# Moving one channel group of a causal depthwise convolution from VectorE to GpSimd, and one transpose to another PSUM bank

## The chip, the cores and the metric

The kernel runs on one core of a Trainium2 chip. The metric is the device time of one execution in microseconds (us). Before the change it is 969.46 us, the median of three runs (969.19 to 971.21). All arithmetic is float32.

## The reference, cut to what matters

The program is one sequence of 256 tokens with 1024 features through two blocks. The first has two residual layers: an mLSTM mixer, then attention, each followed by a feed-forward part with a short convolution. The change doesn't touch it. The second block has two layers of this form, and the change is in them:

```python
p = h @ w_in[l]
u_val, u_gate, g_conv, c_q, c_kv, k_idx, w_idx, g_attn = split(p)
# convolution branch, 512 channels
a = u_val * sigmoid(u_gate)
y = conv_general_dilated(a, conv_w, causal, CONV_WIDTH=31, depthwise) + conv_b
y = silu(layernorm(y)) @ w_pw2
# attention branch: an indexer scores every key, top 64 keys are kept
cq = rmsnorm(c_q); q = cq @ w_uq; q_idx = cq @ w_qidx
score = einsum("bth,bths->bts", w_b, relu(q_idx @ k_idx))
_, sel = top_k(score, 64)            # then softmax attention over sel
x = x + gate * rmsnorm(concat([y_conv * silu(g_conv), y_attn * silu(g_attn)]) @ w_out)
```

The depthwise convolution is a sum over 31 taps: for each channel, y[t] = bias + sum over j of w[j] * a[t - 30 + j].

## The kernel before, in words

Every engine has a program of its own, written out by hand; they are ordered only by semaphores (`S(name)`). An activation lies in SBUF with the features on 128 partitions and the 256 tokens along the free dimension, so the 512 convolution channels are four groups (CC = 4) of 128x256 numbers, `b_a[:, c, :]` for the gated input (with 30 columns of zeros ahead) and `b_y[:, c, :]` for the sum.

**The convolution.** ScalarE makes tap 0 with the bias (`tap0`, L897, semaphore `conv0_done`). VectorE makes the other 30 taps of each group, one `scalar_tensor_tensor` each, b_y = b_a shifted * weight column + b_y (`taps`, L2509). Each tap of a group waits for the one before of the same group. `taps((0, 1), 7)` runs seven rounds, and each round issues a tap of group 0 and one of group 1, so that two chains alternate. These calls fill the places between the steps of the attention branch in VectorE's program (from L2540 to L2572), and the last taps of groups 2 and 3 stand between the eight heads of attention.

**The attention branch on the way.** In one layer TensorE's order is: the value and gate products of groups 0 and 1 (`glu`, L1598 and L1617), c_q (L1043), c_kv with the index keys by tokens (L1647) with the sum of squares of c_q between (L1061), then the products of groups 2 and 3 (`glu` again). In the middle of those stands `turn_kidx` (L1627), which turns the 64 index-key features from tokens to features, twice, into PSUM bank 6. Bank 6 is also where the sum of squares of c_q is. VectorE reads it to make the normalised c_q (`b_cqn`, L2551, semaphore `cqn_done`), so `turn_kidx` waits for `cqn_done`. Next come `turn_kv` (L1635), the products of `b_cqn` with w_uq (L1043), the value heads (L1670), the index scores (L1681) and the gate products (L1043, L1700).

VectorE then folds the index scores over heads (L2588), finds the 64 largest per query in 8 rounds (L2597, L2601), and adds masks to the scores of each head (L2610, L2636), which ScalarE exponentiates (L861) and scales (L853) and TensorE turns (L1773). After the last tap VectorE adds the four groups of b_y for the mean (L2660).

**GpSimd** runs four memsets at the start and nothing more. They count up the semaphore `preset`.

**Loads** are issued by SyncE (and a few by ScalarE); no DMA is in the diff.

Of the kernel before, what the change touches and what calls it, by code (L numbers as in the profile page):

```python
# [18 lines left out]
ALU = mybir.AluOpType  # L19
ACT = mybir.ActivationFunctionType  # L20
AX = mybir.AxisListType

P = 128
T = 256
# [3 lines left out]
EPS = 1e-6  # L28
# [6 lines left out]
DEPTH = 2  # L35
D_CONV, TAPS = 512, 31
CC = D_CONV // P
# [5 lines left out]
NEG = -1e30  # L43
# [76 lines left out]
def model(nc, I, out):  # L120
    with ExitStack() as ctx:
# [5 lines left out]
        def S(name):  # L127

            if name not in sems:
                sems[name] = ctx.enter_context(nc.semaphore(name))  # L130
            return sems[name]
# [4 lines left out]
        work = sb("work", [P, 6 * 2048])  # L136
# [5 lines left out]
        ones = sb("ones", [P, T])  # L142
# [5 lines left out]
        sml = sb("sml", [P, 192])  # L148
        mod = sb("mod", [P, DEPTH, 24])
        cact = sb("cact", [P, 8])  # L150
        pb = [ctx.enter_context(nc.psum_tensor(f"bank{i}", [P, 512], F32)) for i in range(8)]

        def W(a, b):
            return work[:, a:b]
# [6 lines left out]
        def col(name, i):  # L161

            return cols[:, bass.ds(COLS[name][0] + i, 1)]

        def three(ap, n):
            return ap.rearrange("p (a b) -> p a b", a=n)

        ident = pc("ident", P)
# [9 lines left out]
        m_gw = W(8192, 8704).rearrange("p (k n) -> p k n", k=DC)  # L178
# [81 lines left out]
        b_kvtok = three(fr[:, 11616:12016], TB)  # L260
# [3 lines left out]
        b_kidx = W(768, 1024)  # L264
# [5 lines left out]
        b_a = W(6144, 6144 + CC * (T + TAPS - 1)).rearrange("p (c t) -> p c t", c=CC)  # L270
        b_y = three(W(7300, 8324), CC)
        b_z = three(W(8324, 9348), CC)
        b_sg = three(W(9348, 9860), 2)
        b_vals = three(W(10240, 11264), TB)
        b_ysq = three(W(0, 1024), CC)
# [25 lines left out]
        def slot(n):  # L301
            return ring[:, place(n), :]
# [80 lines left out]
        def logs(l, i):  # L383

            return 4 + 4 * l + (0, 1, 2, None, 3)[i] + 1

        def root_no(l, i):

            return 7 + 6 * l + (0, 1, 2, None, 3, 4)[i]
# [11 lines left out]
        def _(sp):  # L401
# [47 lines left out]
                    sp.dma_start(slot8(n)[:, wide * m:wide * (m + 1), :], w[:, wide * m:wide * (m + 1), :])                        .then_inc(S(sem), 16)  # L449
            for n in (2, 3):  # L450
                load(n)
            sp.wait_ge(S("preset"), 3)
            w = I["a_w_in"][0].rearrange("(k p) n -> p k n", p=P)
            sp.dma_start(m_gw[:, :, 0:4], w[:, :, 3072:3076]).then_inc(S("gw_in"), 16)
            sp.dma_start(m_gw[:, :, 32:36], w[:, :, 3076:3080]).then_inc(S("gw_in"), 16)
# [72 lines left out]

        @block.gpsimd
        def _(pool):  # L530
            nc.gpsimd.memset(ones[:, :], 1.0).then_inc(S("preset"), 1)
            nc.gpsimd.memset(sml[:, 180:181], EPS).then_inc(S("preset"), 1)
            nc.gpsimd.memset(m_gw[:, :, :], 0.0).then_inc(S("preset"), 1)
            nc.gpsimd.memset(work[0:8, 12160:12288], NEG).then_inc(S("preset"), 1)

        @block.scalar
        def _(act):
# [87 lines left out]
                .then_inc(S("rows_done"), 1)  # L625
            root(0, 1, 1, pb[2][:, 0:T], D)
            act.wait_ge(S("rows_done"), 1)
            act.wait_ge(S("preset"), 4)
            act.dma_start(scratch.ap(), work[0:8, 11904:12288]).then_inc(S("rows_out"), 16)

            def v_first_out(p):
# [244 lines left out]
            def layer(l):  # L876
# [63 lines left out]
                act.wait_ge(S("ln_done"), logs(l, KV))  # L940
                guess(root_no(l, KV), kv_log, kv_root)
                act.wait_ge(S("kv_turned"), 2 * l + 1)
                nc.scalar.activation(b_kidx, pb[6][:, 0:T], ACT.Copy).then_inc(S("kidx_out"), 1)

                tables(SIGMOID)
                for c in range(2):
# [85 lines left out]
        def _(pe):  # L1032
            mm = nc.tensor.matmul
# [36 lines left out]
                return lambda k: pe.wait_ge(S("xg_ready"), base + k + 1)  # L1070


            pe.wait_ge(S("preset"), 1)
            def idle(n):

                for _ in range(n):
# [18 lines left out]
            for k in range(DC):  # L1095
# [5 lines left out]
                for c in range(2):  # L1101
                    last = mm(pb[0][:, T * c:T * (c + 1)], slot8(0)[:, k, P * c:P * (c + 1)], xg[:, k, :],  # L1102
                              start=(k == 0 and c == 0), stop=(k == DC - 1), skip_group_check=True)
            last.then_inc(S("product"), 1)
            pe.wait_ge(S("preset"), 2)
            pe.wait_ge(S("h_ready"), 1)
            for k in range(DC):
                if k % 4 == 0:
# [44 lines left out]
            for c in range(2):  # L1153
                by_features(0, c, K_BANK[c], (2,)).then_inc(S("three_done"), 1)
                last = by_features(0, c, K_BANK[c], (3, 4, 5))
# [6 lines left out]
            for k in range(DC):  # L1162
                o = 64 * (k % 2)
# [414 lines left out]
            def layer(l):  # L1578
# [42 lines left out]
                def turn_kidx():  # L1621

                    pe.wait_ge(S("cq_out"), 5 * l + 5)
                    pe.wait_ge(S("cqn_done"), l + 1)
                    for b in range(TB):
                        for o in (0, 64):
                            last = mm(pb[6][o:o + 64, P * b:P * (b + 1)], b_kvtok[:, b, 128:192], ident,  # L1627
                                      start=True, stop=True, skip_group_check=True)
                    last.then_inc(S("kv_turned"), 1)

# [24 lines left out]
                turn_kv()  # L1655
                arrived(pe, n + 6)
                pe.wait_ge(S("small_in"), 32 * (l + 1))
                w_uq = slot(n + 6).rearrange("p (k n) -> p k n", k=2)
                for m, bank in enumerate((7, 0, 1, 2)):
                    if m in (1, 3):  # L1660
# [164 lines left out]
        def _(dve):  # L1825
# [9 lines left out]
            def after(n):  # L1835
                dve.wait_ge(S("dve_step"), n)

            def then(ins):

                after(link(ins))  # L1840
# [642 lines left out]
            def layer(l):  # L2483
# [16 lines left out]
                def taps(channels, rounds):  # L2500

                    for _ in range(rounds):
                        for c in channels:
                            tap = done_taps[c] = done_taps[c] + 1
                            if tap == 1:
                                dve.wait_ge(S("conv0_done"), CC * l + c + 1)
                            else:
                                after(marks[c])
                            marks[c] = link(v.scalar_tensor_tensor(  # L2509
                                b_y[:, c, :], b_a[:, c, tap:tap + T], col("conv_w_2", 124 * l + 4 * tap + c),  # L2510
                                b_y[:, c, :], ALU.mult, ALU.add))
# [25 lines left out]
                if l == 0:  # L2537
                    modulation(1, 4, 6)
                    layer_gains(1)
                taps((0,), 4)  # L2540
                glu_raw(1)
                taps((0, 1), 6)

                dve.wait_ge(S("cq_out"), 5 * l + 1)
                v.tensor_tensor(sq[:, 1, :], sq[:, 1, :], sq[:, 0, :], ALU.add).then_inc(S("sum_done"), 1)
                taps((0, 1), 7)
                mean_square(logs(l, CQ), pb[6][:, 0:T], ms[:, 0:T], 256)
                newton(root_no(l, CQ), ms[:, 0:T], rbc, nwt[:, 0:T])
                dve.wait_ge(S("cq_out"), 5 * l + 2)
# [1 line left out]
                    ins = v.scalar_tensor_tensor(b_cqn[:, c, :], b_cq[:, c, :], col("q_norm_g_2", 2 * l + c), rbc,  # L2551
                                                 ALU.mult, ALU.mult)
                ins.then_inc(S("cqn_done"), 1)
                taps((0, 1), 7)
                dve.wait_ge(S("cq_out"), 5 * l + 5)
                v.tensor_scalar(wcol, b_kvtok[:, :, 192:200], IDX_HEADS ** -0.5 * D_IDX ** -0.5, None, ALU.mult)\
                    .then_inc(S("wcol_done"), 1)
# [3 lines left out]
                    ins = v.tensor_scalar(kv_diag[:, b, :], ident, kv_root[:, b:b + 1], None, ALU.mult)  # L2561
                ins.then_inc(S("kvn_done"), 1)
                glu(2)
                taps((0, 1, 2), 4)
                taps((0, 2), 2)
                taps((1, 2), 2)
                glu(3)
                dve.wait_ge(S("kv_turned"), 2 * l + 2)
                v.tensor_scalar(b_kvn, pb[5][:, 0:T], col("kv_norm_g_2", l), None, ALU.mult).then_inc(S("kvn_done"), 1)
                taps((1, 3), 4)  # L2570
                taps((2, 3), 7)
                taps((3,), 3)  # L2572
                dve.wait_ge(S("wcol_done"), l + 1)
# [53 lines left out]
                for n_head in range(8):  # L2627
                    if n_head < 8:
                        h = 8 * (1 + l) + n_head
                        dve.wait_ge(S("am_done"), 4 * l + n_head // 2 + 1)  # L2630
                        dve.wait_ge(S("scores_done"), h + 1)
                        if n_head >= 2:
                            dve.wait_ge(S("exp_done"), 2 * (h - 1))
                        x, at = sc_sb[n_head % 2], 136 + 2 * (n_head % 2)
                        for b, (lo, hi) in enumerate(((0, P), (P, DIAG))):
                            ins = v.tensor_tensor_reduce(x[:, lo:hi], pb[n_head % 2][:, lo:hi], am[:, n_head, lo:hi],  # L2636
                                                         -KV_LORA ** -0.5, 3.4e38, ALU.add, ALU.min,
                                                         sml[:, at + b:at + b + 1])
                        ins.then_inc(S("max_done"), 1)
                    if n_head < 8 and n_head % 2 == 0 and n_head < 6:  # L2640
                        masked_bias(n_head // 2 + 1)
                    if n_head == 0:
                        reciprocals(0)
                        taps((2, 3), 1)
                    elif n_head < 5:
                        taps((2, 3), 2)
                        if n_head == 4:
                            gate_attention(0)
                        reciprocals(n_head)
                    elif n_head < 7:  # L2650
                        if n_head == 6:
                            gate_attention(1)
                        taps((2, 3), 2)
                        reciprocals(n_head)
                        taps((2, 3), 1)
                    else:
                        taps((3,), 1)
                        reciprocals(7)
                        after(marks[3])
                        then(v.tensor_tensor(b_ysq[:, 0:2, :], b_y[:, 0:2, :], b_y[:, 2:4, :], ALU.add))  # L2660
                v.tensor_tensor(b_ysq[:, 0, :], b_ysq[:, 0, :], b_ysq[:, 1, :], ALU.add)\
                    .then_inc(S("sum_done"), 1)
                gate_attention(2)
                assert done_taps == [TAPS - 1] * CC
                dve.wait_ge(S("ss_done"), sums_on_pe(l, MEAN))
                mean = pb[2][:, 0:T].unsqueeze(1).broadcast_to([P, CC, T])
                v.scalar_tensor_tensor(b_yn, mean, -1.0 / D_CONV, b_y, ALU.mult, ALU.add)\
# [111 lines left out]
```

## Time and profile before

| | |
|---|---|
| median of 3 runs | 969.46 us |
| the profiled execution, its own time | 971.52 us |
| its span, first to last instruction | 969.7 us |
| mean granted TensorE clock | 0.998 |
| first of the two layers | from about 690 us to 829 us |
| second | from about 829 us to the end |

Times in the rows further down are microseconds from the start of the span. PE is TensorE, DVE VectorE, ACT ScalarE, POOL GpSimd. The end of a matmul is modelled, and successive matmuls overlap, so a group's start-to-start distance says more than its end: 16 matmuls of 128x256 take 3.45 us from one group's start to the next, though each group is shown with 3.62. The same holds for VectorE: a tap is shown with some 0.48 us, but 14 taps of two alternating groups take 5.62.

### The profile page before, as it was taken

To read this page: it belongs to the slowest core of one execution; us is meant where nothing else is said; L and a number is where in the kernel's file an instruction comes from. 1 tells how busy PE (TensorE), PEld (TensorE's weight loads), DVE (VectorE), ACT (ScalarE), POOL (GpSimd) and SP (SyncE) were. 2 spreads that over 40 slices of the span, in tenths; PEclk is the share of its full clock that TensorE was granted. 3 is DMA by queue.
4 is the path that set the end of the run, shared out by engine and by line. 5 is a ranking of instruction groups with operands and counts; after the bars stand their busy time and mean duration, and the time that the engine had idled before them with its cause. 6 is when DMAs were issued, how large, how long until landed. Compare 5 with 4: busy or idle time off the path is not lost.

```text
span 969.7 us, 15791 instructions
## 1 busy us (share of the span) xinstructions
PE 960.0 (99%) x6003; PEld 871.1 (90%) x6003; DVE 723.1 (75%) x1551; ACT 276.4 (29%) x603; POOL 1.1 (0%) x8
## 2 busy tenths in 40 slices
PE   9999999999999999999999999999999999999997
PEld 8888999999999988888999999999888878888876
DVE  5578777876887489757678778875799972799963
ACT  2133112112111222253121121112433363634561
POOL 0000000000000000000000000000000000000000
PEclk9999999999999999999999999999999999999999
DMA  9891566766776240685357677762753512543201
GB/s 276 276 290 50 180 209 199 264 235 221 256 260 237 70 148 1 193 262 196 122 192 265 216 244 251 270 209 92 227 170 130 163 44 84 190 136 107 63 1 44
DMA packets 132952, 170.72 MB, mean 176 GB/s; under 512 B 8723, under 2 KB 120483, under 8 KB 132771
## 3 DMA queue, kind: packets, MB, share of 16 engines
q1 hardware_dynamic: 131155, 167.69, 52.7%
q10 hardware_dynamic: 1744, 2.32, 0.7%
q8 instruction: 34, 0.56, 0.2%
q14 instruction: 19, 0.16, 0.0%
HBM read 168.93 MB, written 2.64 MB: 177 GB/s over the span
## 4 chain that ended last, share of the span: by engine, by line
PE 95%; DVE 4%; ACT 1%; issue 0%; DVEq 0%; POOL 0%; POOLq 0%
PE bank L1391 26%; PE bank L1404 16%; PE bank L1043 9%; PE bank L1714 5%; PE bank L1501 5%; PE bank L1130 4%; PE bank L1367 3%; PE bank L1700 3%; PE bank L1137 3%; PE bank L1327 3%; PE bank L1617 2%; PE bank L1598 2%; DVE work L2509 2%; PE bank L1054 1%; PE bank L1541 1%; PE bank L1102 1%
## 5 line engine op out<-in xcount | busy, mean ns | idle before, releaser
L1404 PE MATMUL bank<-work,fring 128*128 128x256 f32 x704 | 155.6, 379 | 0.0
L1404 PEld LDWEIGHTS bank<-work,fring 128*128 128x128 f32 x704 | 132.1, 190 | 17.0
L2280 DVE SCALAR_TENSOR_TENSOR work<-work,cols 128x256 f32<-128x256 f32 x176 | 71.6, 479 | 53.2 <-ACT work L723 53.2
L2509 DVE SCALAR_TENSOR_TENSOR work<-work,cols 128x256 f32<-128x256 f32 x240 | 98.8, 477 | 1.0 <-ACT work L897 0.5
L1391 PE MATMUL bank<-sq,fring 128*128 128x128 f32 x640 | 84.5, 275 | 0.0
L723 ACT ACTIVATE work<-work,cols 128x256 f32<-128x256 f32 x88 | 45.6, 589 | 122.1 <-DVE work L2259 100.7
L1391 PE MATMUL bank<-sq,ring 128*128 128x128 f32 x640 | 78.0, 275 | 0.0
L1391 PE MATMUL bank<-ring,fring 128*128 128x128 f32 x640 | 78.0, 275 | 0.0
L1391 PEld LDWEIGHTS bank<-sq,fring 128*128 128x128 f32 x640 | 77.9, 192 | 0.0
L1391 PEld LDWEIGHTS bank<-ring,fring 128*128 128x128 f32 x640 | 76.2, 192 | 1.0
L1391 PEld LDWEIGHTS bank<-sq,ring 128*128 128x128 f32 x640 | 74.7, 192 | 0.0
L2295 DVE SCALAR_TENSOR_TENSOR work<-work,cact 128x1536 f32<-128x1536 f32 x32 | 58.1, 1815 | 0.6
L1714 PE MATMUL bank<-ring,fring 128*128 128x256 f32 x256 | 57.8, 380 | 0.0
L1714 PEld LDWEIGHTS bank<-ring,fring 128*128 128x128 f32 x256 | 48.3, 190 | 6.7 <-issue 0.3
L717 ACT ACTIVATE work<-bank 128x128 f32<-128x128 f32 x40 | 10.8, 275 | 149.5 <-PE bank L1391 149.5
L2256 DVE TENSOR_TENSOR work<-work,bank 128x256 f32<-128x256 f32 x40 | 16.8, 421 | 35.2 <-PE bank L1391 34.2
L1043 PE MATMUL bank<-work,ring 128*128 128x256 f32 x192 | 42.4, 379 | 0.0
L1043 PE MATMUL bank<-xg,ring 128*128 128x256 f32 x192 | 42.3, 380 | 0.0
L1391 PE MATMUL bank<-ring 128*128 128x128 f32 x320 | 42.3, 275 | 0.0
L1043 PEld LDWEIGHTS bank<-xg,ring 128*128 128x128 f32 x192 | 36.3, 190 | 5.1
L1043 PEld LDWEIGHTS bank<-work,ring 128*128 128x128 f32 x192 | 36.3, 190 | 4.9
L1391 PEld LDWEIGHTS bank<-ring 128*128 128x128 f32 x320 | 38.9, 192 | 0.0
(408 smaller groups left out, 1605.5 us busy)
## 6 DMA issues: line engine op xcount, KB each, us to landing
fring<-in_f_w_up SPq DMA_DIRECT2D x44, 1024.0 KB, 7.5
work<-in_w_ada SPq DMA_DIRECT2D x32, 768.0 KB, 6.1
fring<-in_f_w_down SPq DMA_DIRECT2D x22, 1024.0 KB, 5.0
ring<-in_w_in SPq DMA_DIRECT2D x18, 1024.0 KB, 5.3
ring<-in_a_w_in SPq DMA_DIRECT2D x10, 1024.0 KB, 11.8
ring<-in_w_kv SPq DMA_DIRECT2D x8, 1024.0 KB, 7.2
ring<-in_w_out SPq DMA_DIRECT2D x8, 1024.0 KB, 5.1
ring<-in_a_w_out SPq DMA_DIRECT2D x4, 1024.0 KB, 9.9
```

The lines of the kernel that those rows point to most:

```text
L723: nc.scalar.activation(f_t[v][:, c, :], f_u[:, v, c, 0:T], ACT.Identity, bias=col(f"f_conv_b{f}", n), scale=col(f"f_conv_w{f}", n)).then_i ...
L1043: last = mm(bank[:, T * c:T * (c + 1)], w[:, k, at + P * c:at + P * (c + 1)], x[:, k, :], start=(k == 0), stop=(k == nk - 1))
L1130: last = mm(dst, w[:, k, P * c:P * (c + 1)], x[:, k, :], start=(k == 0), stop=(k == 3))
L1137: last = mm(dst, x[:, k, :], w[:, k, :], start=(k == 0), stop=(k == 3))
L1327: last = mm(bank[:, P * at:P * (at + 1)], w[:, k, P * c:P * (c + 1)], side[:, k, :], start=(k == 0), stop=(k == 3))
L1391: last = mm(bank[:, P * at:P * (at + 1)], w[:, k, P * c:P * (c + 1)], x[:, k, :], start=(k == 0), stop=(k == 3))
L1404: last = mm(pb[m // 2][:, T * (m % 2):T * (m % 2 + 1)], w[:, k, P * m:P * (m + 1)], f_act[:, par, T * k:T * (k + 1)], start=(first and k = ...
L1501: last = mm(places[n], x[:, k, :], w[:, k, :], start=(k == 0), stop=(k == 3))
L1714: last = mm(bank[:, 0:T] if apart else bank[:, T * m:T * (m + 1)], y2[:, k, P * b:P * (b + 1)], slot8(load)[:, k, :], start=(k == 4 and (m ...
L2280: ins = v.scalar_tensor_tensor(f_t[q][:, c, :], f_u[:, q, c, tap:tap + T], col(f"f_conv_w{f}", 44 * tap + n), f_t[q][:, c, :], ALU.mult, A ...
L2295: ins = v.scalar_tensor_tensor(acc, f_ada[:, half, :], k, acc, ALU.mult, ALU.add)
L2509: marks[c] = link(v.scalar_tensor_tensor(b_y[:, c, :], b_a[:, c, tap:tap + T], col("conv_w_2", 124 * l + 4 * tap + c), b_y[:, c, :], ALU.m ...
```

## The change

Four edits.

1. GpSimd takes all 30 taps of group 0 in each of the two layers. It has no one-instruction form of a tap here: it multiplies the shifted input by the weight column, broadcast along the tokens, into a scratch row `b_tap`, and adds that to `b_y[:, 0, :]`. Each of the two waits for the other before it. It starts when ScalarE has made tap 0 of group 0. VectorE waits for the last of them ahead of the sum for the mean.
2. VectorE's calls of `taps` lose group 0. Where it stood alone the call is gone; where it stood beside group 1, group 1 now runs alone; two taps of group 1 move ahead.
3. `turn_kidx` writes to bank 4 instead of 6, ScalarE copies from there, and the wait for `cqn_done` moves from `turn_kidx` to the first product that reads `b_cqn`.
4. The semaphore `preset` is called `pool_done`, and goes on counting.

```diff
+        b_tap = W(11920, 12176)
+        def pool_taps(l, tap):
+            return 4 + 2 * (TAPS - 1) * l + 2 * tap
...
+            for l in range(DEPTH):
+                pool.wait_ge(S("conv0_done"), CC * l + 1)
+                for tap in range(1, TAPS):
+                    if tap > 1:
+                        pool.wait_ge(S("pool_done"), pool_taps(l, tap - 1))
+                    nc.gpsimd.tensor_tensor(b_tap, b_a[:, 0, tap:tap + T],
+                                            col("conv_w_2", 124 * l + 4 * tap).broadcast_to([P, T]),
+                                            ALU.mult).then_inc(S("pool_done"), 1)
+                    pool.wait_ge(S("pool_done"), pool_taps(l, tap) - 1)
+                    nc.gpsimd.tensor_tensor(b_y[:, 0, :], b_y[:, 0, :], b_tap, ALU.add).then_inc(S("pool_done"), 1)
...
                 act.wait_ge(S("kv_turned"), 2 * l + 1)
-                nc.scalar.activation(b_kidx, pb[6][:, 0:T], ACT.Copy).then_inc(S("kidx_out"), 1)
+                nc.scalar.activation(b_kidx, pb[4][:, 0:T], ACT.Copy).then_inc(S("kidx_out"), 1)
...
                     pe.wait_ge(S("cq_out"), 5 * l + 5)
-                    pe.wait_ge(S("cqn_done"), l + 1)
...
-                            last = mm(pb[6][o:o + 64, P * b:P * (b + 1)], b_kvtok[:, b, 128:192], ident,
+                            last = mm(pb[4][o:o + 64, P * b:P * (b + 1)], b_kvtok[:, b, 128:192], ident,
...
                 pe.wait_ge(S("small_in"), 32 * (l + 1))
+                pe.wait_ge(S("cqn_done"), l + 1)
...
-                taps((0,), 4)
                 glu_raw(1)
-                taps((0, 1), 6)
+                taps((1,), 6)
...
-                taps((0, 1), 7)
+                taps((1,), 7)
                 mean_square(logs(l, CQ), pb[6][:, 0:T], ms[:, 0:T], 256)
...
-                taps((0, 1), 7)
+                taps((1,), 7)
                 dve.wait_ge(S("cq_out"), 5 * l + 5)
...
                 glu(2)
-                taps((0, 1, 2), 4)
-                taps((0, 2), 2)
-                taps((1, 2), 2)
+                taps((1, 2), 8)
                 glu(3)
...
-                taps((1, 3), 4)
+                taps((1, 3), 2)
+                taps((3,), 2)
                 taps((2, 3), 7)
                 taps((3,), 3)
...
                         after(marks[3])
+                        dve.wait_ge(S("pool_done"), pool_taps(l, TAPS - 1))
                         then(v.tensor_tensor(b_ysq[:, 0:2, :], b_y[:, 0:2, :], b_y[:, 2:4, :], ALU.add))
```

## Rows read from the trace of the kernel before

**Rows 1.** The page: busy time, share of the span and instructions of each engine.

```profile
PE 960.0 (99%) x6003; PEld 871.1 (90%) x6003; DVE 723.1 (75%) x1551; ACT 276.4 (29%) x603; POOL 1.1 (0%) x8
```

**Rows 2.** TensorE's waits, whole span: who waited for whom, total, times, longest.

```profile
PE bank L1627 <- DVE work L2551: 1.2, 1, 1.2
...
PE bank L1773 <- ACT sq L853: 0.6, 2, 0.3
```

**Rows 3.** TensorE in order of time: start, duration, line, tile, shape, count [idle before].

```profile
714.15 0.59 PE L1061 MATMUL bank<-sq,ones 128*128 128x256 f32 x2
...
717.29 3.62 PE L1598 MATMUL bank<-xg,ring 128*128 128x256 f32 x16
722.08 0.66 PE L1627 MATMUL bank<-consts,fring 128*64 128x128 f32 x8 [1.18 <-DVE work L2551]
...
733.14 0.61 PE L1635 MATMUL bank<-ms,fring 128*128 128x128 f32 x4
733.58 7.07 PE L1043 MATMUL bank<-work,ring 128*128 128x256 f32 x32
...
858.03 3.62 PE L1598 MATMUL bank<-xg,ring 128*128 128x256 f32 x16
861.75 0.66 PE L1627 MATMUL bank<-consts,fring 128*64 128x128 f32 x8
```

**Rows 4.** ScalarE in order of time, first layer.

```profile
700.64 0.58 ACT L897 ACTIVATE work<-work,cols 128x256 f32<-128x256 f32 x1
...
718.01 0.50 ACT L934 ACTIVATE fring<-bank 128x400 f32<-128x400 f32 x1
...
746.92 1.08 ACT L967 ACTIVATE fring<-bank 128x512 f32<-128x512 f32 x2 [0.88 <-PE bank L1681]
```

**Rows 5.** VectorE in order of time, first layer.

```profile
704.81 2.05 DVE L2509 SCALAR_TENSOR_TENSOR work<-work,cols 128x256 f32<-128x256 f32 x4
...
713.35 0.41 DVE L2545 TENSOR_TENSOR sq<-sq 128x256 f32<-128x256 f32 x1
713.69 5.62 DVE L2509 SCALAR_TENSOR_TENSOR work<-work,cols 128x256 f32<-128x256 f32 x14
...
721.06 0.88 DVE L2551 SCALAR_TENSOR_TENSOR work<-work,cols,rstd 128x256 f32<-128x256 f32 x2
721.85 5.62 DVE L2509 SCALAR_TENSOR_TENSOR work<-work,cols 128x256 f32<-128x256 f32 x14
...
728.25 0.48 DVE L2561 TENSOR_SCALAR ms<-consts,sml 128x128 f32<-128x128 f32 x2
...
747.89 0.48 DVE L2588 SCALAR_TENSOR_TENSOR fring<-fring,consts 128x256 f32<-128x256 f32 x1
...
752.14 0.35 DVE L2588 SCALAR_TENSOR_TENSOR fring<-fring,consts 128x128 f32<-128x128 f32 x1
```

**Rows 6.** The taps (L2509) by stretch: length, VectorE busy (count), granted clock, DMA.

```profile
700.00:748.00 48.00, 36.35 (x89) 1.00 0.49 154
839.00:888.00 49.00, 36.33 (x89) 1.00 0.46 151
...
766.00:790.00 24.00, 13.04 (x31) 1.00 0.34 108
```

**Rows 7.** GpSimd's instructions by form: busy, mean ns.

```profile
L533 POOL MEMSET work<- 128x512 f32 x1 | 0.5, 524 | 0.0
L531 POOL MEMSET ones<- 128x256 f32 x1 | 0.3, 312 | 0.3 <-POOLq L2767 0.3
```

**Rows 8.** The first layer's attention in order of time: TensorE, ScalarE, VectorE.

```profile
773.52 0.49 PE L1773 MATMUL bank<-consts,sq 128*128 128x128 f32 x3
...
790.96 0.55 PE L1773 MATMUL bank<-consts,sq 128*128 128x128 f32 x3 [0.31 <-ACT sq L853]
...
771.98 0.80 ACT L853 ACTIVATE sq<-sq,sml 128x128 f32<-128x128 f32 x2 [0.15 <-DVE sml L2625]
...
789.96 0.67 DVE L2660 TENSOR_TENSOR work<-work 128x512 f32<-128x512 f32 x1
```

More of the change, by code:

```diff
@@ L451, in _ @@
                 load(n)
-            sp.wait_ge(S("preset"), 3)
+            sp.wait_ge(S("pool_done"), 3)
             w = I["a_w_in"][0].rearrange("(k p) n -> p k n", p=P)
@@ L530, in _ @@
         def _(pool):
[L531 to L534, printed above, removed]
+            nc.gpsimd.memset(ones[:, :], 1.0).then_inc(S("pool_done"), 1)
+            nc.gpsimd.memset(sml[:, 180:181], EPS).then_inc(S("pool_done"), 1)
+            nc.gpsimd.memset(m_gw[:, :, :], 0.0).then_inc(S("pool_done"), 1)
+            nc.gpsimd.memset(work[0:8, 12160:12288], NEG).then_inc(S("pool_done"), 1)
+            for l in range(DEPTH):
[8 more added lines that the diff above has]
+                    nc.gpsimd.tensor_tensor(b_y[:, 0, :], b_y[:, 0, :], b_tap, ALU.add).then_inc(S("pool_done"), 1)
         @block.scalar
@@ L627, in _ @@
             act.wait_ge(S("rows_done"), 1)
-            act.wait_ge(S("preset"), 4)
+            act.wait_ge(S("pool_done"), 4)
             act.dma_start(scratch.ap(), work[0:8, 11904:12288]).then_inc(S("rows_out"), 16)
@@ L1070, in xg_ready @@
                 return lambda k: pe.wait_ge(S("xg_ready"), base + k + 1)
-            pe.wait_ge(S("preset"), 1)
+            pe.wait_ge(S("pool_done"), 1)
             def idle(n):
@@ L1104, in _ @@
             last.then_inc(S("product"), 1)
-            pe.wait_ge(S("preset"), 2)
+            pe.wait_ge(S("pool_done"), 2)
             pe.wait_ge(S("h_ready"), 1)
@@ L2663, in layer @@
                 gate_attention(2)
-                assert done_taps == [TAPS - 1] * CC
+                assert done_taps == [0] + [TAPS - 1] * 3
                 dve.wait_ge(S("ss_done"), sums_on_pe(l, MEAN))
```

## The prediction, made before the changed kernel ran

> **What bounds the kernel now.** I start at the busy times. TensorE is at 99% and VectorE at 75% [rows 1], and a quarter of free VectorE time might tempt one to look there; but with TensorE full, an edit can give back only TensorE's waits. So the second view is TensorE's waits. In the two layers that the change touches there are three kinds. One is the wait of `turn_kidx` for the normalised c_q, once, 1.2 us. Another is a wait of the head transposes for ScalarE, 0.6 us over two places [rows 2]. The third, between the layers and at the end, waits on the output norm and isn't touched.
>
> The third view is TensorE in order of time, because a wait shown after a modelled end is a little too short. In the first layer L1598 starts at 717.29, and 16 matmuls take 3.45 from start to start, so `turn_kidx` could start at 720.74. It starts at 722.08: 1.34 us are lost. In the second layer it could start at 861.48 and starts at 861.75: 0.27 lost [rows 3]. That is all the time that edit 3 can give: 1.6 us.
>
> VectorE's order of time tells why it can matter though it is not full. Its taps run without a gap to 747.89, where folding the index scores starts [rows 5]; ScalarE's first relu, which that step needs, started at 746.92 and holds two of 0.54 [rows 4]. So VectorE reaches the index about 0.4 us after its input is there. From there the top-64 search and the eight heads follow at once. In the heads TensorE turns a head at 773.52 that ScalarE finished scaling at 772.78 [rows 8]. So VectorE may be late at the index by some 0.7 us, and each further microsecond makes TensorE wait. VectorE is a second bound, hidden under the first.
>
> **The change, part by part.** The rename (edit 4) costs nothing: the same counts at the same instructions.
>
> *Edit 3, the other bank.* Without the wait for `cqn_done`, `turn_kidx` needs only the copy of c_kv, which ends at 718.51 [rows 4], before 720.74. Bank 4 was read before that copy. The moved wait stands ahead of the product at 733.58 (732.24 once the stall is gone) [rows 3]; b_cqn is ready at 721.94 [rows 5], so 10 us cover it. Behind it on TensorE stand all later products, so if the cover went, each microsecond would count in full. Gain: 1.34 + 0.27 = 1.6 us, if all else keeps pace.
>
> *Edit 2, what VectorE saves.* 89 taps stand ahead of the index in each layer [rows 6]; 30 of them go. Two prices are needed. A tap in a single chain costs 0.51 (2.05 for 4), a tap in alternating chains 0.40 (5.62 for 14) [rows 5]. Before: 4 single, and 12, 14, 14, 20 and 25 alternating. After: 0, then 6, 7 and 7 single, 16 alternating, and 23 of which 2 are newly single. Savings: 2.0; 4.8 - 3.1 = 1.7; 5.6 - 3.6 = 2.0 twice; 8.0 - 6.4 = 1.6; 10.0 - 9.4 = 0.6. In sum 9.9 us a layer. Alone they bring almost nothing: VectorE would wait for groups 2 and 3 and then for the relu, whose time TensorE sets. The 31 shown in the attention stretch stay.
>
> *Edit 1, GpSimd's own time.* 60 instructions a layer, each waiting for the one before. The trace has no such instruction; the nearest are memsets, 0.312 us at 256 columns and 0.524 at 512 [rows 7], or 0.10 fixed and 0.21 per 256 columns of one stream. Estimate: at least 0.31 (all streams at once), at most 0.73 (two read and one written in turn); I take 0.52, the two reads in turn, and 0.1 for the semaphore step. The chain starts at about 701.2, when tap 0 is made [rows 4], and is needed at 789.96 [rows 8]: 88.8 us for 60, or 1.48 each. Even 0.73 plus the step stays under it; undisturbed, the chain ends near 701.2 + 60 * 0.62 = 738. The wait added on VectorE (behind it: the mean, the layer norm, the last gates) should cost nothing.
>
> *Edit 1, what it does to VectorE.* This is the disputed term. Every tap on VectorE reads two tensors from SBUF, and so do most other instructions between 701 and 748. Nothing in this trace has both engines busy in SBUF. Bound from below: 0, if they don't disturb each other. Bound from above, 0.73 - 0.13 = 0.60 us for each GpSimd instruction: VectorE stands for all of the slowest one, less what it can hide. The 0.13 comes from VectorE's prices: 0.48 at 256 columns and 0.35 at 128 [rows 5] make 0.27 of streaming in the 0.40 of a tap, so 0.13 of each tap is not streaming. With my 0.52 the price is 0.39.
>
> The trace shows only that GpSimd has been silent beside VectorE [rows 7]. The Trainium skill (SBUF — State Buffer, "Who interferes with whom") says that a VectorE instruction with two SBUF inputs contends with a GpSimd instruction that reads SBUF, and "SBUF: two separate sides" calls it an exclusive lock for the whole instruction. No row here shows it. By that rule the sum is the 0.39 to 0.60 case below; without it the 0 case. The skill's GPSIMD Engine Reference, "Elementwise — side-by-side cycle accounting", has about 2.6 cycles an element for two inputs; 256 of them at 1.2 GHz would be an estimated 0.55 us, beside my 0.52.
>
> At what price does the loss begin? 9.9 us saved, over up to 60 instructions that fall ahead of the index, is 0.165 us each. Any disturbance above a sixth of a microsecond makes VectorE later at the index than now. I think some disturbance likely, since a tap needs two streams at once from a memory whose access the two engines might share, and take turn-taking as likeliest. The sum per layer: some 6 of the 60 fall beside VectorE instructions that read at most one SBUF tensor (reduces, bank reads, some 5.5 us), leaving 54 * 0.39 = 21.1; the 20 single taps already had 0.12 of waiting each that this fills, -2.4; less 9.9 saved; less the 0.7 that the heads lend. That leaves 8.1 us late, and twice that is 16 us. TensorE waits for it ahead of the heads, so the 1.6 us of edit 3 are swallowed there. 971.5 + 16 = 987.5 for the profiled execution; its own time stood 2 us over the median, so I predict 985.5.
>
> **On the way** the same price would show at two places earlier. The sum of squares (L2545) has 17 disturbed instructions ahead: +6.6 - 3.7 saved = 716.2 instead of 713.35, and TensorE needs it at 714.15 [rows 3, 5], a wait of over 2 us. kv_diag (728.25 plus 0.4) would come near 736, needed at 733.14. Both stalls only anticipate the one at the index.
>
> **The rivals.**
>
> *A. No disturbance.* For: nothing in the rows speaks of one. Then VectorE has b_cqn at about 719 and waits for TensorE at groups 2 and 3, edit 3 gives its 1.6 us, and the head stalls (0.47 each: eight matmuls of 0.216 from 788.76 leave TensorE free at 790.49, it starts at 790.96 [rows 8]) stay, as they come from the heads' own chain. 969.5 - 1.6 = 967.9; with both head stalls 967.0.
>
> *B. A mild disturbance, each slowed a bit.* At 0.1 us each VectorE still reaches the index in time, giving 968; at 0.3, 54 * 0.3 - 2.4 - 9.9 - 0.7 = 3.2 us a layer, or 976. I put the case at 968 to 980.
>
> *C. VectorE keeps the path and GpSimd starves.* Back-to-back taps leave it only gaps. It decides from 1.48 us per GpSimd instruction; at 1.8 the chain ends 19 us late, less some 8 us of products that cover it: +11 a layer, 991. Against it: VectorE's dependent single taps leave a gap after every one.
>
> *D. Turn-taking at the upper price, 0.60:* 54 * 0.60 - 2.4 - 9.9 - 0.7 = 19.4 a layer, 1008.
>
> **Chances.** Turn-taking at about 0.39, D with it: 0.45. C: 0.07. B: 0.23 (above the 0.2% bound 0.10, within it 0.10, below 0.03). A: 0.25 (faster by over 0.2%, which is 1.9 us and about what a measurement of this kernel can tell from no change, 0.11; within it 0.14, since 1.6 lies just inside). So faster 0.14, same 0.24, slower 0.62. Most chance lies on one side, but A is a quarter, so the range must reach it: 966.8 to 1008, leaving out half of D. The likeliest case's own range is 976 to 1008.
>
> **What would show it.** Right: L2509's mean between 705 and 760 grows from 0.48 to 0.7 or more while POOL is busy and falls back once POOL is done; the index (L2588) starts some 9 us later relative to L1681; a new wait of TensorE for VectorE of about 8 us ahead of or in the heads. The GpSimd chain ends well before L2660. Edit 3 is right if L1627 has no wait and the wait at the b_cqn product is nil. Wrong: L2509 at 0.48 with POOL busy (then A), or VectorE waiting ahead of L2660 for POOL (then C). A VectorE gap ahead of groups 2 and 3 would also speak for A.

## The result, and the profile after

The changed kernel takes 991.02 us (median of 4, 989.56 to 992.26) beside 970.34 us for the kernel before in the same session (969.19 to 971.33): a ratio of 1.0208 with a 95% interval of 1.0191 to 1.0226, or 20.2 us of 970.34 (the two medians are 20.7 apart). The forecast was 985.5 us, in a range from 966.8 to 1008, and slower. Its profiled execution has a span of 987.8 us, but the layers began 2.4 us earlier in that execution than in the one before (the first product of the layer at 687.76 instead of 690.19), before anything of the change has run. Counted from the start of the layers the difference is 987.8 - 969.7 + 2.4 = 20.5 us.

The page of the changed kernel, part 1, against [rows 1]: TensorE has much the same work, VectorE has 60 instructions less and 18 us **more** busy time.

```profile
PE 963.5 (98%) x6003; PEld 872.1 (88%) x6003; DVE 741.1 (75%) x1491; ACT 276.5 (28%) x603; POOL 88.3 (9%) x128
```

Part 5 of the same page, three of its groups. A tap (L2525, formerly L2509) is now 0.632 us on the mean of the whole kernel instead of 0.48:

```profile
L546 POOL TENSOR_TENSOR work<-work,cols 128x256 f32<-128x256 f32 x60 | 40.3, 672 | 803.5 <-ACT work L913 798.9
...
L2525 DVE SCALAR_TENSOR_TENSOR work<-work,cols 128x256 f32<-128x256 f32 x180 | 105.3, 632 | 3.2 <-ACT work L913 1.3
...
L550 POOL TENSOR_TENSOR work<-work 128x256 f32<-128x256 f32 x60 | 46.8, 781 | 4.7
```

TensorE's waits, against [rows 2]. The wait at `turn_kidx` is gone. A larger one has come, at the c_q products, for VectorE's gating of the fourth group (L2532):

```profile
PE bank L1059 <- DVE work L2532: 14.6, 2, 7.4
...
PE bank L1059 <- DVE mod L2209: 0.7, 1, 0.7
...
PE bank L1059 <- ACT hT L922: 0.5, 1, 0.5
```

TensorE in order of time, first layer and then the same place of the second, against [rows 3]. L1642 is `turn_kidx`; it follows at once. L1059 at 731.02 is the product of c_q with w_uq: 24 matmuls run, then TensorE stands for 7.37 us, and the last 8 take 3.58 from start to start where 8 took 1.73:

```profile
719.37 0.66 PE L1642 MATMUL bank<-consts,fring 128*64 128x128 f32 x8
...
730.48 0.71 PE L1650 MATMUL bank<-ms,fring 128*128 128x128 f32 x4
731.02 5.34 PE L1059 MATMUL bank<-work,ring 128*128 128x256 f32 x24
743.73 3.78 PE L1059 MATMUL bank<-work,ring 128*128 128x256 f32 x8 [7.37 <-DVE work L2532]
747.31 4.12 PE L1059 MATMUL bank<-work,fring 128*128 128x256 f32 x16
751.27 1.88 PE L1686 MATMUL bank<-fring,work 128*128 128x512 f32 x4
...
881.16 5.34 PE L1059 MATMUL bank<-work,ring 128*128 128x256 f32 x24
893.69 3.78 PE L1059 MATMUL bank<-work,ring 128*128 128x256 f32 x8 [7.19 <-DVE work L2532]
897.27 4.24 PE L1059 MATMUL bank<-work,fring 128*128 128x256 f32 x16
901.34 1.88 PE L1686 MATMUL bank<-fring,work 128*128 128x512 f32 x4
```

The reason for those slow 8 is in the windows of the two stretches after the waits (length, busy of PE, PEld, DVE, ACT, POOL, then the granted clock): 0.70 and 0.69 of full speed on the mean, so part of each at the lower level, 1.2 GHz, after TensorE had stood for 7 us. It was 1.00 at the same work before [rows 6].

```profile
743.00:752.00 9.00, 8.27 (x26) 6.66 (x27) 8.93 (x19) 3.79 (x7) 3.71 (x6) 0.70 0.36 116
893.00:902.00 9.00, 8.31 (x26) 6.72 (x27) 8.93 (x19) 3.72 (x7) 3.67 (x6) 0.69 0.35 116
```

VectorE in order of time, first layer, against [rows 5], and then GpSimd beside it:

```profile
706.28 4.88 DVE L2525 SCALAR_TENSOR_TENSOR work<-work,cols 128x256 f32<-128x256 f32 x6 [0.67 <-ACT work L913]
711.08 0.95 DVE L2560 TENSOR_TENSOR sq<-sq 128x256 f32<-128x256 f32 x1
711.96 5.68 DVE L2525 SCALAR_TENSOR_TENSOR work<-work,cols 128x256 f32<-128x256 f32 x7
...
729.50 0.92 DVE L2576 TENSOR_SCALAR ms<-consts,sml 128x128 f32<-128x128 f32 x2
730.34 0.41 DVE L2532 TENSOR_TENSOR work<-bank,work 128x256 f32<-128x256 f32 x1
730.68 12.67 DVE L2525 SCALAR_TENSOR_TENSOR work<-work,cols 128x256 f32<-128x256 f32 x16
743.27 0.41 DVE L2532 TENSOR_TENSOR work<-bank,work 128x256 f32<-128x256 f32 x1
743.60 0.47 DVE L2582 TENSOR_SCALAR work<-bank,cols 128x256 f32<-128x256 f32 x1
743.99 11.53 DVE L2525 SCALAR_TENSOR_TENSOR work<-work,cols 128x256 f32<-128x256 f32 x23
755.44 0.48 DVE L2602 SCALAR_TENSOR_TENSOR fring<-fring,consts 128x256 f32<-128x256 f32 x1
```

```profile
731.09 0.67 POOL L546 TENSOR_TENSOR work<-work,cols 128x256 f32<-128x256 f32 x1
731.84 0.79 POOL L550 TENSOR_TENSOR work<-work 128x256 f32<-128x256 f32 x1
732.70 0.68 POOL L546 TENSOR_TENSOR work<-work,cols 128x256 f32<-128x256 f32 x1
...
746.31 0.79 POOL L550 TENSOR_TENSOR work<-work 128x256 f32<-128x256 f32 x1
```

Seven single-chain taps take 5.68 us, 0.81 each; sixteen in alternating chains take 12.67, 0.79 each; a pair of GpSimd instructions starts every 1.61, 0.81 each. The two engines run in lock step in these stretches, one tap to one GpSimd instruction, whatever the chain. The gating at 730.34, one of whose inputs is in PSUM, keeps its 0.41 in the middle of it. Once GpSimd is through (746.31 + 0.79 = 747.1), the taps are back at 0.40 and the top-64 search and the heads are as before. The index starts 67.7 us after the layer's first product, where it started 57.7 after (747.89 - 690.19): 10.0 us late.

### The profile page after: what moved, and what is told of

Same layout as the page of the kernel before. It is cut to its first block, busy times and chain, and to the rows that moved or that the text cites. A ratio compares the mean times of both kernels' runs of the same rounds, so it can differ in the third digit from the quotient of the medians.

```text
span 987.8 us, 15857 instructions
## 1 busy us (share of the span) xinstructions
PE 963.5 (98%) x6003; PEld 872.1 (88%) x6003; DVE 741.1 (75%) x1491; ACT 276.5 (28%) x603; POOL 88.3 (9%) x128
## 3 DMA queue, kind: packets, MB, share of 16 engines
HBM read 168.93 MB, written 2.64 MB: 174 GB/s over the span
## 4 chain that ended last, share of the span: by engine, by line
PE 88%; DVE 10%; ACT 1%; issue 1%; DVEq 0%; POOL 0%; POOLq 0%
PE bank L1407 25%; PE bank L1420 15%; PE bank L1059 8%; DVE work L2525 5%; PE bank L1730 5%; PE bank L1517 5%; PE bank L1146 4%; PE bank L1383 3%; PE bank L1716 3%; PE bank L1343 3%; PE bank L1153 2%; PE bank L1070 1%; PE bank L1557 1%; DVE xg L2509 1%; PE bank L1614 1%
## 5 line engine op out<-in xcount | busy, mean ns | idle before, releaser
L546 POOL TENSOR_TENSOR work<-work,cols 128x256 f32<-128x256 f32 x60 | 40.3, 672 | 803.5 <-ACT work L913 798.9
L2296 DVE SCALAR_TENSOR_TENSOR work<-work,cols 128x256 f32<-128x256 f32 x176 | 71.6, 479 | 53.2 <-ACT work L739 53.2
L2525 DVE SCALAR_TENSOR_TENSOR work<-work,cols 128x256 f32<-128x256 f32 x180 | 105.3, 632 | 3.2 <-ACT work L913 1.3
L1059 PE MATMUL bank<-work,ring 128*128 128x256 f32 x192 | 46.5, 402 | 14.6 <-DVE work L2532 14.6
L1730 PE MATMUL bank<-ring,fring 128*128 128x256 f32 x256 | 57.7, 380 | 0.0
L1059 PEld LDWEIGHTS bank<-work,ring 128*128 128x128 f32 x192 | 38.3, 202 | 20.9 <-DVE work L2532 15.4
L550 POOL TENSOR_TENSOR work<-work 128x256 f32<-128x256 f32 x60 | 46.8, 781 | 4.7
L1059 PE MATMUL bank<-xg,ring 128*128 128x256 f32 x192 | 42.5, 381 | 1.2 <-DVE mod L2209 0.7
L2272 DVE TENSOR_TENSOR work<-work,bank 128x256 f32<-128x256 f32 x40 | 16.8, 421 | 35.0 <-PE bank L1407 34.1
L1059 PEld LDWEIGHTS bank<-xg,ring 128*128 128x128 f32 x192 | 36.1, 190 | 7.0 <-DVE mod L2209 1.1
```

What stands on the lines that cost most here:

```text
L546: nc.gpsimd.tensor_tensor(b_tap, b_a[:, 0, tap:tap + T], col("conv_w_2", 124 * l + 4 * tap).broadcast_to([P, T]), ALU.mult).then_inc(S("po ...
L550: nc.gpsimd.tensor_tensor(b_y[:, 0, :], b_y[:, 0, :], b_tap, ALU.add).then_inc(S("pool_done"), 1)
L1059: last = mm(bank[:, T * c:T * (c + 1)], w[:, k, at + P * c:at + P * (c + 1)], x[:, k, :], start=(k == 0), stop=(k == nk - 1))
L1730: last = mm(bank[:, 0:T] if apart else bank[:, T * m:T * (m + 1)], y2[:, k, P * b:P * (b + 1)], slot8(load)[:, k, :], start=(k == 4 and (m ...
L2296: ins = v.scalar_tensor_tensor(f_t[q][:, c, :], f_u[:, q, c, tap:tap + T], col(f"f_conv_w{f}", 44 * tap + n), f_t[q][:, c, :], ALU.mult, A ...
L2525: marks[c] = link(v.scalar_tensor_tensor(b_y[:, c, :], b_a[:, c, tap:tap + T], col("conv_w_2", 124 * l + 4 * tap + c), b_y[:, c, :], ALU.m ...
```

## The experiments

All ratios are against the kernel before, on the same chip.

**1. The other bank alone.** Edit 3 on the kernel before (the two hunks of `turn_kidx` and the copy, and the moved wait).

> The kernel before with the other bank for the index keys and the moved wait alone; VectorE keeps all taps, GpSimd does nothing. My theory (the two engines take turns at SBUF and the 20 us come from that) expects 1.34 + 0.27 = 1.6 us less than before, ratio 0.9983, L1627 without a wait. A rival (the moved wait, or bank 4, is what costs: the stall moves to the c_q product) expects no gain or a loss.

Measured 0.9985 (0.9976 to 0.9995), and no wait at `turn_kidx`. The gain is 1.5 us (between 0.5 and 2.3 by the interval), in line with the 1.6 forecast, and edit 3 is no part of the loss.

**2. VectorE's new order without GpSimd.**

```diff
-            for l in range(DEPTH):
-                pool.wait_ge(S("conv0_done"), CC * l + 1)
...
-                        dve.wait_ge(S("pool_done"), pool_taps(l, TAPS - 1))
```

> The changed kernel without GpSimd's 60 instructions a layer and the wait for them: the 30 taps of group 0 are left out altogether. VectorE's program is that of the changed kernel. My theory (GpSimd's instructions hold VectorE up) expects the whole loss to be gone: taps at 0.48 and 0.51 again, 0 to 1 us beyond the gain of the bank alone, ratio 0.997 to 0.999. The rival (the new order of the taps, with single chains and the second gate product behind 16 taps, costs) expects a part of the 20 us to stay, 1.005 or more.

Measured 0.9982 (0.9972 to 0.9992). The whole loss is GpSimd's doing; and 30 taps fewer on VectorE are worth nothing that can be told from the bank alone. The trace shows why: seven single taps are back at 3.60 us, and VectorE stands for 3.19 us ahead of the index until ScalarE's relu is there.

```profile
710.28 3.60 DVE L2514 SCALAR_TENSOR_TENSOR work<-work,cols 128x256 f32<-128x256 f32 x7
...
744.04 0.48 DVE L2591 SCALAR_TENSOR_TENSOR fring<-fring,consts 128x256 f32<-128x256 f32 x1 [3.19 <-ACT fring L972]
```

**3. GpSimd busy, but only writing.**

```diff
-                for tap in range(1, TAPS):
...
+                for i in range(4 * (TAPS - 1)):
+                    if i > 0:
+                        pool.wait_ge(S("pool_done"), 4 + 4 * (TAPS - 1) * l + i)
+                    nc.gpsimd.memset(b_tap, 0.0).then_inc(S("pool_done"), 1)
```

> The changed kernel with GpSimd's 60 arithmetic instructions a layer replaced by 120 memsets of the scratch row, 128x256 each, one waiting for the other: about as long a chain (120 * 0.4 = 48 us) that writes SBUF but reads nothing; group 0's taps are left out. If the disturbance is in the reading alone, as the Trainium skill has it (SBUF - State Buffer, Who interferes with whom), ratio 0.997 to 0.999, like the run without any. If any GpSimd instruction in SBUF holds VectorE up, a memset of 0.31 takes up to 0.2 from it and 120 of them some 15 us a layer: 1.01 to 1.02.

Measured 0.9979 (0.9969 to 0.9989). VectorE in order of time, beside the memsets: seven single taps in 3.60, where they took 5.68 beside reading instructions.

```profile
706.98 3.09 DVE L2521 SCALAR_TENSOR_TENSOR work<-work,cols 128x256 f32<-128x256 f32 x6 [0.67 <-ACT work L909]
...
712.57 3.60 DVE L2521 SCALAR_TENSOR_TENSOR work<-work,cols 128x256 f32<-128x256 f32 x7
...
722.31 0.36 DVE L1857 TENSOR_SCALAR sml<-sml 128x2 f32<-128x2 f32 x1
```

The memsets ran from 701.23 to 745.6, so both stretches lie beside them. GpSimd's being on, or its writing, does not hold a tap up. What the arithmetic instructions do beyond a memset is read (and calculate); that the reading is the cause is what is left, but no run here has GpSimd read without writing.

**4. Half the GpSimd instructions.** The products are left out, the 30 adds a layer stay.

```diff
-                    nc.gpsimd.tensor_tensor(b_tap, b_a[:, 0, tap:tap + T],
-                                            col("conv_w_2", 124 * l + 4 * tap).broadcast_to([P, T]),
-                                            ALU.mult).then_inc(S("pool_done"), 1)
```

> The changed kernel with GpSimd's products left out: only the 30 adds a layer remain, each reading two rows (the scratch row holds zeros). In turn-taking the price is per instruction: 30 instead of 60 at 0.30 to 0.39 is 9 to 11 us a layer, and VectorE has 9.9 saved, so the loss should be nearly or wholly gone, 0.998 to 1.001. If the loss grew with the time that GpSimd is busy in some other way (a fixed cost of having it on), 1.010.

Measured 1.0011 (1.0001 to 1.0021): the loss shrinks from 20 us to 1, more than by half, because the first 9.9 us a layer are paid for by the saved taps. That is how a price per instruction with a threshold behaves, not a fixed cost. TensorE's wait for the fourth gating is gone; what is left are two small ones ahead of the c_q projection, 0.5 and 0.3. Each add takes somewhat more from a single tap than the mix of products and adds did, 0.87 - 0.51 = 0.36 instead of 0.30:

```profile
712.60 6.15 DVE L2521 SCALAR_TENSOR_TENSOR work<-work,cols 128x256 f32<-128x256 f32 x7
```

**5. The gating ahead of the taps.**

```diff
-                taps((1, 2), 8)
+                taps((1, 2), 2)
                 glu(3)
                 dve.wait_ge(S("kv_turned"), 2 * l + 2)
...
+                taps((1, 2), 6)
```

> The changed kernel with the fourth group's gating product (and the value keys behind it) moved ahead of 12 of the 16 taps of groups 1 and 2. TensorE's 7.4 us wait in each layer stood at the product that needs that gating. If VectorE's total load ahead of the index decides, the wait only moves to the heads: ratio 1.015 to 1.021 against before, and the c_q product without a wait. If the place decides (the bank is released too late), the 7 us a layer are gone: 1.000 to 1.006.

Measured 1.0194 (1.0177 to 1.0212), and TensorE's waits are these instead:

```profile
PE bank L1059 <- ACT work L986: 8.7, 2, 4.4
PE bank L1789 <- ACT sq L869: 4.6, 4, 2.6
```

L1059 is now the gate products behind the index scores, held by ScalarE, which stood 10.66 us for VectorE's folding (L983 at 758.75, first layer); L1789 turns the heads. The wait has moved and stayed, 13.3 us instead of 14.6: VectorE's load ahead of the index is what counts.

**6. The load without the saving.** GpSimd's second instruction writes `b_tap` instead of `b_y`, and VectorE's calls of `taps` are those of the kernel before.

```diff
-                    nc.gpsimd.tensor_tensor(b_y[:, 0, :], b_y[:, 0, :], b_tap, ALU.add)
+                    nc.gpsimd.tensor_tensor(b_tap, b_a[:, 0, tap:tap + T], b_tap, ALU.add)
...
-                taps((1,), 7)
+                taps((0, 1), 7)
```

> The kernel before with the other bank, VectorE making all taps of all groups, and GpSimd running the same 60 instructions a layer into the scratch row alone, so that nobody needs them: the load without the saving. The price per GpSimd instruction by the changed kernel's taps is 0.39 in alternating chains and 0.30 in single ones; here nearly all are alternating: 56 * 0.39 - 0.7 = 21 us a layer later, plus 2 for the half clock after the wait, so 46 us, ratio 1.043 to 1.052. If the saving of 9.9 us a layer in the changed kernel was not real, about the changed kernel's 1.021.

Measured 1.0386 (1.037 to 1.0402), below the expected range of 1.043 to 1.052. From 704.26, where its taps start, VectorE needs 62.2 us to the index instead of 43.1: 19.1 more over the 53 GpSimd instructions that start in it, 0.36 each, as some of them fall beside instructions that they don't disturb. The taps themselves pay the full 0.39: 14 in 11.04 us and 11.13, then 20 in 8.00 once GpSimd is through. With nothing saved, the two early stalls that the prediction names "on the way" do come: over the two layers TensorE waits 9.5 us for the sum of squares (L1077 for L2561) and 16.8 for kv_diag (L1650 for L2577).

```profile
719.04 11.04 DVE L2525 SCALAR_TENSOR_TENSOR work<-work,cols 128x256 f32<-128x256 f32 x14
...
734.01 11.13 DVE L2525 SCALAR_TENSOR_TENSOR work<-work,cols 128x256 f32<-128x256 f32 x14
...
747.51 8.00 DVE L2525 SCALAR_TENSOR_TENSOR work<-work,cols 128x256 f32<-128x256 f32 x20
...
766.42 0.48 DVE L2604 SCALAR_TENSOR_TENSOR fring<-fring,consts 128x256 f32<-128x256 f32 x1
```

**7. Products that read one row.**

```diff
-                    nc.gpsimd.tensor_tensor(b_tap, b_a[:, 0, tap:tap + T],
-                                            col("conv_w_2", 124 * l + 4 * tap).broadcast_to([P, T]),
-                                            ALU.mult).then_inc(S("pool_done"), 1)
+                    nc.gpsimd.tensor_scalar(b_tap, b_a[:, 0, tap:tap + T], col("conv_w_2", 124 * l + 4 * tap),
+                                            None, ALU.mult).then_inc(S("pool_done"), 1)
```

> The changed kernel with the products on GpSimd as tensor_scalar with the weight as a column per partition: one row read instead of two, the same result. If an instruction blocks for its own length, the product should be shorter than 0.67 us (0.4 to 0.5) and VectorE's tap period fall from 0.81 to about 0.70: some 3 us a layer back, ratio 1.012 to 1.016. If the price is per instruction whatever its length, 1.021.

Measured 1.0198 (1.0182 to 1.0214): no better. My expectation was wrong at its start, since with one row to read the product is longer, not shorter. By form:

```profile
L546 POOL TENSOR_SCALAR work<-work,cols 128x256 f32<-128x256 f32 x60 | 60.0, 1000 | 793.3 <-ACT work L912 787.6
...
L549 POOL TENSOR_TENSOR work<-work 128x256 f32<-128x256 f32 x60 | 46.7, 779 | 5.0
```

VectorE's single taps did fall to 0.71 (seven in 4.95), but the chain lasted to 758.5 and ran into the folding of the index scores (seven in 4.56 instead of 3.81). Fifteen alternating taps took 9.41 us instead of 6.03 beside some ten GpSimd instructions, 0.34 each, so the longer product did not raise the price; but it is an instruction of another kind, and the run doesn't separate "per instruction" from "per length". TensorE waited 12.2 us for the head transposes (L1788) here, and only 1.5 for the fourth gating.

**8. GpSimd where VectorE reads one row.** The other bank; of the last taps of groups 2 and 3, seven (three and four) are GpSimd's, started when the index scores are folded, and VectorE's in the heads are fewer by as many.

```diff
+POOL_TAPS = ((3, 0), (2, 0), (3, 1), (2, 1), (3, 2), (2, 2), (3, 3))
...
+            for l in range(DEPTH):
+                pool.wait_ge(S("relu_read"), 6 * l + 6)
+                for i, (c, back) in enumerate(POOL_TAPS):
+                    tap = TAPS - 1 - back
...
-                        taps((2, 3), 2)
+                        taps((2, 3), 7 - n_head)
                         reciprocals(n_head)
-                        taps((2, 3), 1)
                     else:
-                        taps((3,), 1)
                         reciprocals(7)
```

> The kernel before with the other bank, all of VectorE's taps ahead of the index as before, and GpSimd making 7 of the last taps of groups 2 and 3 beside the top-64 search, where VectorE's instructions read one SBUF tensor each (10.8 us, 14 GpSimd instructions of about 0.77). If only instructions with two SBUF inputs are held up, the search stays at its length, and VectorE has 7 taps less between the heads: the 1.6 us of the bank and up to 0.9 of the last head's stalls, ratio 0.997 to 0.9985. If the search is held up too, each of the 14 costs up to 0.39 and the ratio is 1.005 to 1.010.

Measured 0.9973 (0.9963 to 0.9983), 967.72 us: faster than both kernels. GpSimd and VectorE in order of time at the first layer's search:

```profile
755.66 0.61 POOL L545 TENSOR_TENSOR work<-work,cols 128x256 f32<-128x256 f32 x1 [753.98 <-DVE fring L2603]
756.36 0.73 POOL L549 TENSOR_TENSOR work<-work 128x256 f32<-128x256 f32 x1
...
765.35 0.73 POOL L549 TENSOR_TENSOR work<-work 128x256 f32<-128x256 f32 x1
```

```profile
755.62 0.62 DVE L2612 MAX8 fring<-fring 128x8 f32<-128x128 f32 x2
...
757.77 0.41 DVE L2616 MATCH_REPLACE8 fring<-fring 128x256 f32<-128x256 f32 x1
...
766.02 0.36 DVE L2619 TENSOR_SCALAR fring<-fring 128x384 f32<-128x384 f32 x1
```

The search takes 10.40 us from 755.62 to 766.02, the same 10.4 as before, and GpSimd's instructions are shorter, 0.61 and 0.73, one every 0.75. TensorE's wait for the head transposes falls from 0.6 to 0.2, but that for the output norm (L1825 for L2747) grows from 0.5 to 0.9. Against the bank alone (0.9985) the intervals overlap, so a gain of the taps themselves is not shown; this run also changes the place of `reciprocals` among the taps of the last heads.

**9 and 10. The same 14 instructions in two places.** The other bank, all taps on VectorE, and 7 products and 7 adds a layer on GpSimd into the scratch row that nobody needs; one kernel starts them at `relu_read`, the other at `conv0_done` of the third group. The cut shows the one line in which the two differ.

```diff
-                pool.wait_ge(S("relu_read"), 6 * l + 6)
+                pool.wait_ge(S("conv0_done"), CC * l + 3)
```

> The kernel before with the other bank, all taps on VectorE as before, and 14 GpSimd instructions a layer (7 products, 7 adds of group 1's rows into the scratch row, needed by nobody) started when the index scores are folded, beside the top-64 search. If only VectorE instructions that take the shared way are held up, they are free here: the ratio of the bank alone, 0.9985 with its interval of 0.9976 to 0.9995. If any VectorE work is held up, 14 * 0.39 = 5.5 us a layer: 1.008 or more.

> The same kernel as the one with 14 GpSimd instructions beside the search, but started when tap 0 of the third group is made, so that they run beside VectorE's taps in alternating chains. At 0.39 each that is 5.5 us a layer, less 0.7 that the heads lend: 4.8 a layer, 9.5 us in all above the bank alone, ratio 1.006 to 1.009. If the place does not matter, the same as beside the search.

Beside the search 0.9994 (0.9984 to 1.0005), which overlaps with the bank alone; the search took the same 10.4 us. Beside the taps 1.0134 (1.0117 to 1.0151), more than the expected 1.006 to 1.009. The 20 taps of that place:

```profile
729.30 13.51 DVE L2522 SCALAR_TENSOR_TENSOR work<-work,cols 128x256 f32<-128x256 f32 x20
```

They took 8.00, so 5.5 us for 14 instructions: 0.39, as expected. What I had left out is what follows. TensorE waits 5.22 and 4.16 us for the fourth gating and then works at a lower clock, 8 matmuls in 3.58 and 16 in 3.95 (second layer 3.57 and 4.25) instead of 1.73 and 3.45. That is 2.35 and 2.64 us more. The sum, 14.4, is what lies between 0.9985 and 1.0134.

## Why the prediction was right

**Where the 20 us lie.** TensorE's two large gaps, counted from start to start, are 7.54 and 7.36 us (743.73 less 731.02 and 24 matmuls of 0.2155; the second layer alike). The low clock behind them costs 1.85 + 0.51 and 1.85 + 0.62. Two small waits ahead of the c_q projection (4.34 and 4.13 us from the start of the group before, instead of 3.48) add 0.86 and 0.65. Together 21.2; less the 1.6 of edit 3 it is 19.6, of 20.2 by the ratio.

**The disputed term** was 0.39 for each GpSimd instruction, 0.12 less beside single taps. Measured: 0.79 - 0.40 = 0.39 in alternating chains, 0.81 - 0.51 = 0.30 in single ones. The Trainium skill (SBUF — State Buffer, "Who interferes with whom") names the condition under which it happens, two SBUF inputs against a GpSimd instruction that reads. The runs agree with it: writing alone costs the taps nothing (experiment 3), and the search, with one SBUF input each, is free (experiment 8). In the same page the Trainium skill, under "SBUF: two separate sides", calls it an exclusive lock for the whole instruction. The rows show turns being taken, with a period of 0.81. By my estimate 0.27 of that is the tap's streaming [rows 5], so GpSimd would hold it for some 0.54 of the 0.67 to 0.79 that its instructions are shown with; no run measures how long it is held.

**The whole of it** is in line too: the sum had 54 * 0.39 - 2.4 = 18.7 us a layer that GpSimd takes from VectorE; measured are 10.0 late and the 9.9 saved, 19.9.

**GpSimd's own time** was mis-sized: 0.52 + 0.10 forecast, 0.67 and 0.79 with 0.08 between in lock step, 0.75 from start to start undisturbed. The 0.52 was meant as the whole instruction and turned out near the part that blocks, so the price came out right for a partly wrong reason: that it hit 0.39 to the second digit is luck. The chain ended at 747.1 rather than 738, well before it was needed, as said.

**VectorE's lateness at the index** was forecast as 8.1 + 0.7 = 8.8 us; it is 10.0. The saving of 9.9 is borne out by the two prices (0.40 and 0.51) wherever GpSimd is silent.

**Edit 3** gave 1.5 of 1.6 us alone (experiment 1). Inside the change it only brings TensorE earlier to a wait that is longer by as much, so it gives nothing there, also as said.

**What was off.** Three things.

The place: I had TensorE waiting in or ahead of the heads, but it waited earlier, at the last quarter of the w_uq product, which writes a bank that the fourth gating must have read; that gating stood behind 16 slowed taps. By experiment 5 the place doesn't matter for the sum, and in experiment 7 the wait did lie at the heads.

The two early stalls that I named "on the way" did not come: the sum of squares was ready at 712.0, needed at 712.69, and kv_diag at the very moment (730.4 for 730.48). Counted from the layer's first product VectorE was late by 0.2 us at the first of them, where I had 2.9, and by 4.1 at the second, where I had 7.4. I had charged all 17 GpSimd instructions ahead of the sum of squares with 0.39, or 6.6 us. They took 3.5: 1.2 from six `scalar_tensor_tensor` (3.65 instead of 2.46), 0.5 from one of 128x8 (L2229, 0.66 instead of 0.17) and 1.8 from six single taps (4.88 instead of the 3.09 of experiment 3), while the others fell beside reduces, bank reads and waits.

And the clock: I had no term for what TensorE loses after a long wait, 4.8 us in the two layers. With it, 16 would have been 21. This one term is most of what lies between the forecast and the measured time.

**The rivals.** No disturbance (A) is out by the taps at 0.79 to 0.81 and by experiments 2 and 6, which show that the loss comes with GpSimd and grows when nothing is saved. A mild one (B), up to 0.3 for each instruction, is too small for the 0.36 on the mean of experiment 6. Starvation of GpSimd (C) named 991 us, the very time that was measured, but its mechanism is not there: GpSimd kept its pace of 0.81 against 0.75 undisturbed, was through at 747.1, and VectorE did not wait for it ahead of the mean (L2675, at 797.29). The upper price (D) was not reached.

## What to carry to other kernels

Before giving VectorE's work to GpSimd, count not what VectorE saves but what each GpSimd instruction that reads SBUF takes from it: here 0.39 us per instruction of 256 columns, against 0.40 to 0.51 saved for a tap that costs two of them (whether GpSimd could make a tap in one was not tried). The break-even was a sixth of a microsecond. GpSimd cost nothing beside the search for maxima, whose instructions read one SBUF tensor each, and beside a `tensor_tensor` with one input in PSUM; beside `tensor_scalar` from SBUF to SBUF, which also reads only one, it did cost (next section). Whether moving work there gains anything here is open (experiment 8). And a wait of TensorE costs more than its length: after 7 us of standing, 8 matmuls took 3.58 us instead of 1.73 and the next 16 some 4.0 instead of 3.45.

## What the runs showed of the hardware that I had not expected

A GpSimd product with the weight as a per-partition column is slower than one with the same weight broadcast as a second tensor: 1.00 against 0.67 us at 128x256, both beside VectorE's taps (experiment 7). VectorE's `tensor_scalar` from SBUF to SBUF is held up too, though it reads one tensor: two of 128x128 took 0.92 instead of 0.48 beside GpSimd (L2576), while a `tensor_tensor` of 128x256 with one input in PSUM kept its 0.41. Even beside memsets a 128x2 `tensor_scalar` took 0.36 instead of 0.16, and the two of 128x128 took 0.61 (experiment 3). A short instruction pays as much as a long one: a `tensor_tensor` of 128x2 with both inputs in SBUF took 0.57 instead of 0.16 (L1866 at 728.08). With adds alone on GpSimd the lock step had a period of 0.87 (seven single taps in 6.15), set by 0.79 of the add and 0.08 to the next. So in lock step the price is not a constant: it is GpSimd's period less the tap's own pace.
